# Tanh gates in an attention layer, weight splits moved one by one, and modulation pieces placed between projections

## The reference

```python
for i in range(4):
    shift, scale, gate = split(silu(c) @ mod_w[i] + mod_b[i], 3)      # once for context, once for latent
    h = x * (1 + scale) + shift
    # attention (i == 1)
    q, k, v, g = split(h @ attn_w_in)                                 # q, k: RMS norm per head, rotary
    out = (softmax(q k^T / 8) v * silu(g)) @ attn_w_out
    # pooling (i == 2), four groups with windows 2, 4, 8, 16
    u, z = split(h @ pool_w_in, 2)
    out = ((centred_mean(u) - u) @ group_w * scale * silu(z)) @ pool_w_out
    # SSD (i == 0, 3): projections, depthwise convolution with 5 taps, silu, chunked scan, gate by silu(z)
    x = layer_norm(alpha * x + gate * out)
```

## Time and profile before

| | us |
|---|---|
| median of 3 runs | 1648.58 (1648.41 to 1650.85) |
| the profiled execution itself | 1646.72 |
| its span, first to last instruction | 1645.5 |
| PE busy | 1493.8 (91% of the span) |
| DVE busy | 1124.8 (68%) |
| ACT busy | 726.5 (44%) |
| POOL busy | 313.4 (19%) |
| PE's granted clock, mean | 0.95 of full |

### The profile page before, as it was taken

The page is one execution under the profiler, slowest core; times in us unless marked ns, Lnnn a source line. Parts: engine busy times, 40 slices in busy tenths (PEclk is TensorE's granted clock), DMA queues, the critical chain, the costliest instruction groups (busy, mean ns, idle before and its releaser), DMA issues.

```text
span 1645.5 us, 22737 instructions
## 1 busy us (share of the span) xinstructions
PE 1493.8 (91%) x8557; PEld 1231.7 (75%) x8557; DVE 1124.8 (68%) x1712; ACT 726.5 (44%) x1279; POOL 313.4 (19%) x379
## 2 busy tenths in 40 slices
PE   5889999999989998888788899988998989999987
PEld 3768888888768897665568686776888778787876
DVE  0788999999973766456446563454447888888896
ACT  1545555545543534554534322223325545544452
POOL 1043434444420010000001000000001322222340
PEclk7899999999999999999899998999999999999989
DMA  9345554455524122214321435244340343333343
GB/s 310 94 121 153 161 177 132 124 157 154 176 81 154 52 80 91 90 52 154 115 95 36 148 99 188 76 130 154 109 128 3 106 118 113 103 103 102 103 128 128
DMA packets 169421, 197.38 MB, mean 120 GB/s; under 512 B 9696, under 2 KB 151648, under 8 KB 169312
## 3 DMA queue, kind: packets, MB, share of 16 engines
q1 hardware_dynamic: 158480, 163.08, 31.8%
q0 software_dynamic: 9296, 30.19, 6.9%
q10 hardware_dynamic: 1536, 2.67, 0.4%
HBM read 194.59 MB, written 1.31 MB: 119 GB/s over the span
## 4 chain that ended last, share of the span: by engine, by line
PE 48%; DVE 31%; ACT 9%; issue 7%; DMA 2%; SPq 2%; POOL 1%; DVEq 0%; ACTq 0%
PE ps L415 13%; PE ps L416 13%; PE ps L417 13%; DVE xc L894 8%; DVE w_lo L384 5%; DVE cum_b L902 3%; ACT w_hi L377 2%; ACT Wb L766 2%; PE ps L444 1%; PE ps L1843 1%; SPq L2379 1%; DVE Wb L921 1%; DVE Hs L939 1%; ACT xc L735 1%; DMA raw<-in_pool_group_w 1%
## 5 line engine op out<-in xcount | busy, mean ns | idle before, releaser
L415 PE MATMUL ps<-h_hi,w_hi 128*128 128x512 f32 (+2 forms) x1088 | 416.4, 383 | 33.7 <-DVE w_lo L384 29.2
L416 PE MATMUL ps<-h_lo,w_hi 128*128 128x512 f32 (+2 forms) x1088 | 403.5, 371 | 0.0
L417 PE MATMUL ps<-h_hi,w_lo 128*128 128x512 f32 (+2 forms) x1088 | 403.3, 371 | 0.0
L384 DVE TENSOR_TENSOR w_lo<-raw,w_hi 128x1024 fp32r<-128x1024 f32 (+1 forms) x205 | 244.8, 1228 | 137.7 <-ACT w_hi L377 135.9
L377 ACT ACTIVATE w_hi<-raw 128x1024 fp32r<-128x1024 f32 (+1 forms) x205 | 208.6, 1049 | 146.7 <-PE ps L417 123.3
L415 PEld LDWEIGHTS ps<-h_hi,w_hi 128*128 128x128 f32 (+1 forms) x1088 | 209.6, 193 | 80.3 <-issue 44.2
L417 PEld LDWEIGHTS ps<-h_hi,w_lo 128*128 128x128 f32 (+1 forms) x1088 | 208.8, 192 | 34.5
L416 PEld LDWEIGHTS ps<-h_lo,w_hi 128*128 128x128 f32 (+1 forms) x1088 | 209.6, 193 | 31.8
L894 DVE SCALAR_TENSOR_TENSOR xc<-ps,gp,xc 128x508 f32<-128x508 f32 (+1 forms) x224 | 162.5, 728 | 41.9 <-ACT xc L735 36.0
L417 PE MATMUL ps<-w_hi,ylo 128*128 128x512 f32 x384 | 151.5, 395 | 0.0
L415 PE MATMUL ps<-w_hi,h_hi 128*128 128x512 f32 (+1 forms) x336 | 120.7, 359 | 2.6 <-DVE ys L973 1.0
(11 more groups left out here) (259 smaller groups left out, 2642.1 us busy)
## 6 DMA issues: line engine op xcount, KB each, us to landing
raw<-in_mod_w SPq DMA_DIRECT2D x80, 512.0 KB, 4.6
raw<-in_ssm_w_in SPq DMA_DIRECT2D x64, 512.0 KB, 4.7
cum_b<-cum_scratch POOLq DMA_DIRECT2D x96, 256.0 KB, 5.4
raw<-in_ssm_w_in SPq DMA_DIRECT2D x66, 256.0 KB, 4.4
raw<-in_ssm_w_out SPq DMA_DIRECT2D x32, 512.0 KB, 4.5
raw<-in_pool_w_in SPq DMA_DIRECT2D x32, 512.0 KB, 4.4
raw<-in_attn_w_in SPq DMA_DIRECT2D x20, 512.0 KB, 4.1
raw<-in_pool_w_out SPq DMA_DIRECT2D x16, 512.0 KB, 4.7
```

The lines of the kernel that those rows point to most:

```text
L384: dve.tensor_tensor(lo[:, 0:width], raw[:, r % RS, 0:width], hi[:, 0:width].bitcast(F32), ALU.subtract).then_inc(lo_done, 1)
L415: pe.matmul(o, hi_s, hi_m, start=first, stop=False)
L416: pe.matmul(o, hi_s, lo_m, start=False, stop=False)
L417: return pe.matmul(o, lo_s, hi_m, start=False, stop=last)
```

## The change

1. **Attention gates.** ACT makes tanh(g/2) in place of silu(g); a new step `gate_product` on DVE makes (1 + tanh(g/2)) g from it, which is twice silu(g), and `v` is halved when it is copied. Whoever waited for the gate on ACT (`gs_a`) now waits for DVE (`gs_d`). The program then has no table load of ACT in the attention layer, where it had eight.
2. **One split per block.** A table `SPLIT_AT` names ten units with the group and block behind which each is split.
3. **Residual gates and early chunks.** `pe_gate` and `act_gate` are done in two halves, in blocks 0 and 1 of group 3. The high and low parts of output chunks 0 to 3 move from the end of group 2 to the same two blocks. In groups 2 and 3 PE turns a modulation piece behind the probabilities instead of ahead of them.
4. **Early units of layer 2.** Two of the three are loaded and split ahead of output chunks 4 to 7, the third stays behind them.
5. **Pooling.** Modulation pieces stand between the z projections, summed in banks 6 and 7 in turn; ACT splits gw behind the third z tile.
6. **Last SSD layer.** The next x (in the last step z) is split ahead of `taps(3)` on DVE and ahead of the silu of tile 2 on ACT.
7. **Scan factors.** 12 wider copies in place of 31.

```diff
@@ -243,10 +243,10 @@
...
         for c in range(0 if L % 3 == 2 else 4, chunks(L)):
-            if c == 12:
+            if c == (4 if L % 3 == 1 else 12):
                 add_early(L, (0, 1))
             add("w", L, "out", c, 0)
-        add_early(L, (0, 1, 2) if L % 3 == 1 else (2,))
+        add_early(L, (2,))
@@ -1069,12 +1073,16 @@
...
+        next_x = ("x", i + 1) if i + 1 < GRP else ("z", i)
+        if last_layer(L):
+            dve_split2(dve, L, *next_x)
         taps(3)
...
-        dve_split2(dve, L, *(("x", i + 1) if i + 1 < GRP else ("z", i)))
+        if not last_layer(L):
+            dve_split2(dve, L, *next_x)
@@ -1319,21 +1327,24 @@
...
-        def fill(o, src, c, d):
-
-            q = src[:, 64 * c + HEADS * d:64 * c + HEADS * d + HEADS].rearrange("p (g h) -> p g h", h=HG)
-            return dve.tensor_copy(sg[:, :, o:o + HG], q)
-
+
+        def fill(o, src, k0, n=1, step=1):
+            q = src[:, :].rearrange("p (k g h) -> p g k h", g=GRP, h=HG)[:, :, k0:k0 + step * (n - 1) + 1:step, :]
+            return dve.tensor_copy(sg[:, :, o:o + HG * n].rearrange("p g (k h) -> p g k h", h=HG), q)
+
+
+        fill(0, cum, 0, 8)
         for d in range(2):
-            for c in range(NT):
-                fill(8 * c + HG * d, cum, c, d)
-                fill(32 + 16 * d + HG * c, dt, c, d)
-        for n, (c, d) in enumerate(((0, 1), (1, 0), (2, 0), (2, 1), (3, 0), (3, 1))):
-            fill(64 + HG * n, ecum, c, d)
-        for n, (c, d) in enumerate(((0, 0), (1, 1), (1, 0), (0, 1), (2, 0), (3, 1))):
-            fill(88 + HG * n, tail, c, d)
-        for n, (c, d) in enumerate(((1, 0), (0, 1), (2, 0), (3, 1))):
-            fill(112 + HG * n, etot, c, d)
+            fill(32 + 16 * d, dt, d, 4, 2)
...
+        fill(100, tail, 1)
+        fill(104, tail, 4, 2, 3)
+        fill(112, etot, 2)
+        fill(116, etot, 1)
+        fill(120, etot, 4, 2, 3)
@@ -1779,6 +1790,11 @@
...
+
+    SPLIT_AT = {(0, 2): ("q", 3, 0), (0, 3): ("q", 3, 1), (1, 0): ("g", 2, 0), (1, 1): ("g", 2, 1),
+                (1, 2): ("g", 3, 0), (1, 3): ("g", 3, 1), (1, 4): ("out", 0, 0), (1, 5): ("out", 1, 0),
+                (2, 4): ("out", 2, 0), (2, 5): ("out", 3, 0)}
@@ -1884,8 +1900,10 @@
...
             if g == 3:
                 if slot == 0:
-                    pe.wait_ge(s["gs_a"], 8)
-                    pe_gate(pe, L)
+                    pe.wait_ge(s["gs_d"], 8)
+                    pe_gate(pe, L, (0, 1))
+                if slot == 2:
+                    pe_gate(pe, L, (2, 3))
@@ -1895,7 +1913,7 @@
                 if mod_slot(g, slot) is not None:
                     pe.wait_ge(s["turned_a"], 3 * g + 3)
                     mod_sum(mod_slot(g, slot))
-                elif mod_slot(g, slot - 1) is not None:
+                elif g < 2 and mod_slot(g, slot - 1) is not None:
                     pe_mod_turn(pe, L + 1, mod_slot(g, slot - 1), 5, 256)
...
         for g in range(NKV):
...
                 turn_probs(n)
+                if more and g >= 2 and mod_slot(g, 2 * m) is not None:
+                    pe_mod_turn(pe, L + 1, mod_slot(g, 2 * m), 5, 256)
@@ -1952,9 +1972,11 @@
...
-        def gate_silu(g, t):
+        def gate_tanh(g, t):
+
             act.wait_ge(s["g_p"], 3 * g + 1 + 2 * t)
-            act.activation(ys[:, 2 * g + t, :], bank[(4 if g == 0 else 6) + t], ACT.Silu).then_inc(s["gs_a"], 1)
+            act.activation(ys[:, 2 * g + t, :], bank[(4 if g == 0 else 6) + t], ACT.Tanh,
+                           scale=0.5).then_inc(s["th_a"], 1)
...
             act.wait_ge(s["turn_p_"], 3 * g + r + 1)
...
         for b in range(2):
             act.activation(vv[:, 2 * b:2 * b + 2, :].rearrange("p t n -> p (t n)"), bank[2 + b],
-                           ACT.Copy).then_inc(s["v_a"], 1)
+                           ACT.Copy, scale=0.5).then_inc(s["v_a"], 1)
@@ -2004,8 +2026,8 @@
...
                 exps(n)
-                if g == 3 and m == 0:
-                    act_gate(act, L)
+                if g == 3 and m < 2:
+                    act_gate(act, L, (2 * m, 2 * m + 1))
@@ -2016,28 +2038,23 @@
...
-                if g < 2 and m == 3:
-                    act_split2(act, L, ("q", "g")[g], 3)
+                if (g, m) in SPLIT_AT:
+                    act_split(act, L, *SPLIT_AT[g, m])
...
                 if g < 3 and m == 4:
                     turned(g + 1, 0)
-                    gate_silu(g + 1, 0)
-                    gate_silu(g + 1, 1)
-                if m == 5:
-                    if g == 0:
-                        act_split2(act, L, "g", 2)
-                    elif g < 3:
-                        for c in (2 * g - 2, 2 * g - 1):
-                            act_split(act, L, "out", c, 0)
-                if g == 2 and m == 5:
-                    for c in range(4):
+                    gate_tanh(g + 1, 0)
+                    gate_tanh(g + 1, 1)
+                if g == 3 and m < 2:
+                    for c in (2 * m, 2 * m + 1):
                         act_yhi(act, L, c)
         for c in range(4, chunks(L)):
             act_yhi(act, L, c)
+        act_early(act, L, (0, 1))
         for c in range(4, chunks(L)):
             act_split(act, L, "out", c, 0)
-        act_early(act, L, (0, 1, 2))
+        act_early(act, L, (2,))
@@ -2109,9 +2126,16 @@
...
+        def gate_product(g):
+            for t in range(2):
+                c = 2 * g + t
+                dve.wait_ge(s["th_a"], c + 1)
+                dve.scalar_tensor_tensor(ys[:, c, :], ys[:, c, :], 1.0, bank[(4 if g == 0 else 6) + t],
+                                         ALU.add, ALU.mult).then_inc(s["gs_d"], 1)
+
         def gate_o(c):
             dve.wait_ge(s["pv_p"], 3 * c + 3)
-            dve.wait_ge(s["gs_a"], c + 1)
+            dve.wait_ge(s["gs_d"], c + 1)
             dve.tensor_tensor(ys[:, c, :], bank[4], ys[:, c, :], ALU.mult).then_inc(s["og_d"], 1)
@@ -2126,7 +2150,9 @@
...
-        dve_resid(dve, L - 1, range(NT))
+        dve_resid(dve, L - 1, (0, 1))
+        gate_product(0)
+        dve_resid(dve, L - 1, (2, 3))
@@ -2137,6 +2163,8 @@
...
                 maxima(n)
+                if g < 3 and m == 5:
+                    gate_product(g + 1)
...
         gate_o(2 * NKV - 1)
         for c in range(4, chunks(L)):
             dve_ylo(dve, L, c)
+        dve_early(dve, L, (0, 1))
         for c in range(4, chunks(L)):
             dve_split(dve, L, "out", c, 0)
-        dve_early(dve, L, (0, 1, 2))
+        dve_early(dve, L, (2,))
@@ -2215,13 +2238,16 @@
...
                 project(pe, bank[4 + t % 2], (L, "z", (g, t // 2)), t % 2, s["z_p"])
-            if more:
-                for q in range(3):
-                    pe.wait_ge(mod_done, mod_at(L + 1, 3 * g + q))
-                    if g:
-                        pe.wait_ge(s["mix_d"], 4 * g)
-                    pe_mod_sum(pe, L + 1, 3 * g + q, 6)
-                    pe_mod_turn(pe, L + 1, 3 * g + q, 6)
+                if more:
+
+                    if t:
+                        pe_mod_turn(pe, L + 1, 3 * g + t - 1, 6 + (t - 1) % 2)
+                    if t < 3:
+                        if t == 2:
+                            pe.wait_ge(mod_done, mod_at(L + 1, 3 * g + 1))
+                        if g:
+                            pe.wait_ge(s["mix_d"], 4 * g)
+                        pe_mod_sum(pe, L + 1, 3 * g + t, 6 + t % 2)
@@ -2272,10 +2298,10 @@
...
                 act.activation(zs[:, t, :], bank[4 + t % 2], ACT.Silu).then_inc(s["zs_a"], 1)
-            if more:
-                for q in range(3):
-                    act_mod_rows(act, L + 1, 3 * g + q, 6)
-            act_split2(act, L, "gw", g)
+                if t == 2:
+                    act_split2(act, L, "gw", g)
+                if more and t < 3:
+                    act_mod_rows(act, L + 1, 3 * g + t, 6 + t % 2)
@@ -2336,9 +2362,11 @@
...
             if more:
-                for q in range(3):
-                    dve_mod_col(dve, L + 1, 3 * g + q, 6)
+                dve_mod_col(dve, L + 1, 3 * g, 6)
+                dve_mod_col(dve, L + 1, 3 * g + 1, 7)
             dve_split2(dve, L, "gw", g)
+            if more:
+                dve_mod_col(dve, L + 1, 3 * g + 2, 6)```

ScalarE in attention, group 0, from block 4's exponentials to the end of block 5. `pr` are probabilities, `prT` turned ones, `ys` at L1957 the gates and at L1963 turned keys and queries. Before:

```order
L1971 ACTIVATE pr,smx<-ps,smx 128x512 x2
L1981 ACTIVATE prT<-ps 128x512 x2
L1963 ACTIVATE ys<-ps 128x512
L1957 ACT_TABLE_LOAD
L1957 ACTIVATE ys<-ps 128x512 x2
L1971 ACT_TABLE_LOAD
L1971 ACTIVATE pr,smx<-ps,smx 128x512 x2
L1963 ACTIVATE ys<-ps 128x512 x2
L1981 ACTIVATE prT<-ps 128x512 x2
```

49 lines of the change are left out of this document (26 added, 23 removed).

## The result

The changed kernel takes 1601.79 us in the median of four runs (1598.84 to 1605.86); the kernel before, on the same chip, 1648.49. The ratio is 0.9725, 95% interval 0.9705 to 0.9745: faster by 2.7%, 46.7 us. The forecast was 1587, with a range of 1573 to 1611. The profiled execution took 1598.84 us with a span of 1597.6, so against the profiled execution before (1646.72) the gain is 47.9 of the 61.4 forecast. This execution is the fastest of the four; by the medians the gain is 46.7. Which 13.5 us are missing, and why, is what the experiments are about.

A forecast was written before the change was run, and what follows sets the result against it. PE, busy 91% of the span, was taken as the bound; 19.7 + 21.7 + 18.1 + 1.9 = 61.4 off the profiled 1646.7 gives 1585.3, and with 1.9 for the median 1587; 8 in 10 range 1573 to 1611.

The forecast's parts named there:

- Attention: Attention layer: hand-overs, modulation turn, residual gates and early unit gain, the start loses; 18.1 us, bounds 9 and 26.
- (a): Attention hand-overs, blocks 4 and 5 of groups 0 to 2: 2.6, 1.5, 1.5 and 2.0 for half clock, 7.6 us.
- (d): Last early unit in attention: its load is freed earlier, so DVE begins 3.4 earlier, plus 1.8 half clock; 5.2 us.
- (b): Residual gates in attention: halves in two blocks with copies behind them; of 7.6 us waiting 1.3 stays, 6.3 gained.
- (c): Attention's modulation turn moves behind the probabilities, PE then waits for DVE's divide; 1.0 of the 3.0 us gained.
- (e): Start of attention: DVE waits for the second gate, norm of q 2.6 later, second product 3.3; 2.0 us lost.
- Pooling: Pieces between z projections shorten the gaps by 12.9 us and raise the clock by 6.8; 19.7 us, bounds 6 and 29.
- Last layer: Earlier split in the last layer lets PE start earlier, 3.1 us in each of seven steps; 21.7 us, bounds 10 and 27.
- Scan factors: Fewer, wider copies of scan factors, twice in the program, gain 1.0 each; 1.9 us, bounds 0 and 3.
- VectorE does take back part: Rival: last layer's period falls by 1.5 only, pooling stalls in each group; gain 33 us, time 1615; chance 0.19.
- The table switch: Rival in attention: each load hid as much again, so (a)'s waits vanish, 12 instead of 5.6; time 1581, chance 0.05.
- The z stream: Rival in pooling: small matmuls and stalls keep PE at the lower clock, 82 us lost; time 1669, chance 0.02.

The follow-up runs named there:

- e8: Changed kernel, in attention ScalarE splits ahead of copying the turned probabilities of the same step, at all ten places; 1590.68 us, ratio 0.9653.
- e6: Changed kernel, at attention's start VectorE takes gate_product(0) between norm_sum(1) and norm_scale(1), residual of tiles 2 and 3 behind q 2's split; 1599.43 us.
- e3: Changed kernel, in pooling VectorE splits the second z unit one tile earlier, after tile 2 in place of tile 3; 1586.45 us, ratio 0.9624.
- e1: Changed kernel with the last layer's split of the next x put back behind C's taps on VectorE and silu(3) on ScalarE; 1617.44 us, ratio 0.9807.
- e4: Changed kernel, in the last layer ScalarE computes the second x tile's centre tap ahead of the eight dt products; 1583.73 us, ratio 0.9609.
- e5: Changed kernel, in attention ScalarE copies turned K and Q tiles earlier; 1603.08 us, ratio 0.9726.
- e11: Changed kernel with the second x tile's centre tap ahead of the dt products in both scan layers, layer 0 too; 1578.17 us, ratio 0.9575.

## Why the prediction was right, and where it was too high

The sign was right, the time lies within the range but 15 us above the forecast, and no stage was slower. The order of the parts was not right: attention, forecast as the third, gave most, and pooling least of the three. By the steps:

- **Attention, 18.1 forecast, 18.2 measured**, with errors that cancel. The row for the whole of attention before answers to the one shown with e8:

```profile
570.50:908.50 338.00, 298.65 (x2147) 240.34 (x2145) 186.57 (x387) 160.55 (x329) 22.50 (x17) 0.94 0.28 88
```

PE's waits gave 13.6 us and its clock 4.5, where the forecast had 3.8 for the clock (2.0 in (a), 1.8 in (d)). (a) The hand-overs' waits went from close to 4.0 to 1.27, 1.06 + 2.06 and 1.11 + 2.05, so by 2.7, 0.9 and 0.8 where I had 2.6, 1.5 and 1.5. (b) The gates' 7.6 went; 1.56 and 0.26 stay in front of the probabilities. (c) failed: the turn moved, but PE then waited 3.54 for `pr`, more than the 3.0 before. I had put that wait at 2; e8 takes 1.1 us off it, so that much is DVE held by a split that waits for ACT, and the rest stays open. (d) The wait of 4.9 is 0.49. (e) The start lost 3.2 (137.6 to 140.7) and not 2.0. By the letter this is one of the things that I said would prove me wrong, a wait of over 2 us ahead of group 0: it is there with 4.1, and e6 shows it to be worth 3.4 to 4.3. Two things stood in no term: a wait of 2.0 for a modulation load in group 1 is new, and of PE's waits before, 1.7 for `pr` in groups 0 and 1 and 1.1 for rows in groups 2 and 3 are gone.
- **Pooling, 19.7 forecast, 13.9 measured.** The mechanism was the forecast one, late raw slots in every group; the stalls were 1.5, 1.3, 2.7 and 4.4 and not 0.8, 0.8, 1.5 and 3.7: 9.9 in place of 6.8. What I did not put into the sum is that a stall in the z stream lowers the clock of the projection behind it, 4.2 us over the four groups (e3). I had counted the clock only as a gain. Together these are 3.1 + 4.2 = 7.3 us, more than the 5.8 that are missing, so the other terms were sized 1.5 too low; and e3, which removes both, comes to 13.9 + 14.2 = 28.1, beside my bound of 29 for no stalls.
- **Last layer, 21.7 forecast, 14.9 by e1.** From x projection to x projection the step fell from 39.3 to 36.7, 2.6 and not 3.1: the idle of DVE before the first taps went as forecast, but it came back as 2.5 in place of about 1.5 before the second taps, because ACT had the tap behind products that wait for DVE. The row of before, in the same step as the idle of 2.34 in the earlier trace rows:

```profile
1349.79 3.10 DVE L894 SCALAR_TENSOR_TENSOR xc<-ps,gp,xc 128x508 f32<-128x508 f32 x4 [1.46 <-ACT xc L735]
```

That is the sentence "after that it never waits in this part"; it was read from one place and not from the whole step. And in the last step the earlier start ran into y, L555 waiting 4.65: up to the start of the last z projection the part gave 19.2 us (374.5 from the end of pooling, 393.7 in e1), and from there to the end it gave back 4.4 (71.2 us, 66.8 in e1).
- **Scan factors, 1.9 forecast.** There were 32 copies and one of the skip factors, 33 in all and not 32, and now there are 13; "31" in the description of the kernel and "19 copies fewer" in the forecast are one short. In the last layer they take 1.5 us, from 1263.52 to 1265.05, in place of 2.9. But DVE then waits 0.85 for ACT's high part, so the next split begins 2.38 us behind the taps where it began 2.94 behind them; in layer 0 it is 1.82 and 2.95. That is 1.7 on DVE over both layers, so the size is right. What of it reaches the total isn't shown: layer 0 ends 0.6 earlier, less than the 5 us by which equal layers 0 differ.
- **The rivals.** VectorE does take back part, in the last layer by its second hole and in pooling by its late split; all that is missing is 13.5 us of 61.4, and that rival had 28. The table switch costs its row: had a load hidden as much again, (a) would have come out near 12. The z stream stayed at full clock but for three projections behind stalls; so the small matmuls do not lower it, the stalls in front of them do, as e3 shows, where the same small matmuls stand without stalls at 5.78 us a projection.

## What to carry to other kernels

When a chain is taken out between an engine and the one that feeds it, list that feeder's waits over the whole period, not at the place of the edit: the hole that was hidden moves to the next wait, and it was worth as much again here (e4, 15 us, by moving one ACT instruction in each step). Where a wait goes and the time stays (e5), compare PE's busy time for the same matmuls as well. A wait too short to be listed still counts when it recurs in every step (e11, 0.4 us each). Price a new stall twice where rows of the same kernel show it: once for itself and once for the clock of the work behind it (here 9.9 and 4.2 us).
